# The first sum of every Strassen quarter on GpSimd instead of VectorE, in a one-core encoder trunk

## The chip, the cores and the metric
One core of one Trainium2 chip runs the whole program. The time is device microseconds (us) of one execution. The kernel before took 1798.45 us, the median of 3 runs (1797.22 to 1799.62).

## The reference, cut to what matters
The program computes a two-layer encoder trunk on x of shape (1, 256, 2048), all in float32: layer 0 is a pooling mixer and an MLP, then shared keys and values are made, layer 1 is a differential attention and an MLP, and a last normalization follows. The change lies in the two MLPs alone:

```
def sqrelu_mlp(h, w_in, w_out):        # h (1, 256, 2048)
    u = jax.nn.relu(h @ w_in)          # w_in  (2048, 8192)
    return (u * u) @ w_out             # w_out (8192, 2048)

for l in range(2):
    ...
    h = h + sqrelu_mlp(rms_norm(h, mlp_norm[l]), w_mlp_in[l], w_mlp_out[l])
```

Each MLP streams 134 MB of weights from HBM, and each weight is used for 256 tokens.

## The kernel before, in words
**Tiles.** The 8192 hidden columns of an MLP are cut into NP = 8 pairs of two strips of 512. For pair 0 the product h @ w_in is made plainly. For pairs 1 to 7 it is made by Strassen's scheme in the Winograd form: the tokens (2 x 128), the rows of the weights (two halves) and the columns (two strips) make 2 x 2 blocks, and seven products stand in for eight. Each pair is done in four **units** (k = 0 to 3, the quarters of the inner dimension). A unit loads four pieces a, b, c, d of 128 x 1024 float32 (512 KB each) into `raw_half[0]`. The seven right-hand operands of a unit are a, c, d and four sums, made in place: b = a + b, then d = d + b, a = d - a, c = c + d.

**Exactness.** TensorE multiplies float32r values. So each operand is split into a high part (`w_hi`, a rounding copy by ScalarE, L560 or L566) and a low part (`w_lo = raw - w_hi`, by VectorE, L960), and each product is three matmuls: hi*hi, hi*lo, lo*hi. One 128 x 1024 operand split in this way is a **lot**; `w_hi` and `w_lo` have 8 slots, used in turn. Behind the seven lots of a unit come four lots of `w_out` for the pair before (`out_lot`, two calls, each of which splits two lots: L554 on ScalarE, L952/L954 on VectorE), whose products go to the output.

**Who does what.** SP issues the loads; a and b of the next unit are issued when the sixth lot of this one is split (`in_unit`, L441, L436). ScalarE makes the high parts, seeds and drains PSUM banks. VectorE makes all four sums of a unit (L967, L976, L979, L981), the low parts, the recombinations of Strassen's products (`c_11`, L1051, and `c_rest`, L1057 to L1067) and the low parts of the hidden activations (`u_low`, L1074). TensorE runs the products (L1508 to L1510 into fresh banks, L1514 to L1516 onto seeded ones) and the transposes of the hidden tiles (L1543, once for each pair). GpSimd makes only the reciprocal roots of the norms.

**Order.** Every engine has one list in program order, written by hand, and counters (semaphores) hold it. `lo_ready` counts lots that are split, `pe_done` lots that TensorE has used, `w_summed` the sums. The second sum of a unit (L976) waits for the first by `w_summed`, and so does ScalarE's high part of b (`hi_sum`, L566). On VectorE the first sum (L967) stands at the head of each unit, behind the two `out_lot` calls of the unit before, and in unit 0 behind `c_rest`. On one **round** (one pair), VectorE's list is: c_11 of the pair; out lots; c_rest; first sum, lots and sums of unit 0 with `u_low` between them; out lots; units 1, 2 and 3 in the same way.

Of the kernel before, what the change touches and what calls it, by code (L numbers as in the profile page):

```python
# [26 lines left out]
ALU = mybir.AluOpType  # L27
# [10 lines left out]
RAW = 4  # L38
# [12 lines left out]
NP = FF // (2 * SW)  # L51
# [83 lines left out]
def trunk(nc, x, pool_w, pool_scale, w_kv, w_q, lam, w_o,  # L135
          w_mlp_in, w_mlp_out, final_norm, keep_consts, pool_consts, out):
    with ExitStack() as ctx:
# [3 lines left out]
        def sem(name):  # L141
            return ctx.enter_context(nc.semaphore(name))
# [47 lines left out]
        def place(at, *shape):  # L190
            n = int(np.prod(shape))
            ap = arena[:, at:at + n]
            if len(shape) == 2:
                ap = ap.rearrange("p (a b) -> p a b", b=shape[1])
            if len(shape) == 3:
                ap = ap.rearrange("p (a b c) -> p a b c", b=shape[1], c=shape[2])
            return ap
# [37 lines left out]
        raw_half = (raw, place(0, RAW, 2, SW))  # L235
# [24 lines left out]
        raw_landed = [sem(f"raw_landed{i}") for i in range(2 * RAW)]  # L260
# [27 lines left out]
        w_summed = sem("w_summed")  # L288
# [77 lines left out]
        def i_at(layer, p):  # L366
            if isinstance(p, int) and p == 0:
                return MLP_AT[layer]
            return p * 44 + (MLP_AT[layer] - 28)
# [7 lines left out]
        def i_landed(layer, p, i):  # L377
            if isinstance(p, int) and p == 0:
                return LANDED[layer][i % 2] + i // 2 + 1
            return p * 4 + (LANDED[layer][0] - 2 + i + 1)  # L380
# [133 lines left out]
        @block.gpsimd  # L514
        def _(pool):
            nc.gpsimd.memset(x_ssq[:, :, 0:4], 0.0).then_inc(sums_cleared, 1)
            nc.gpsimd.memset(x_ssq[:, :, 4:5], EPS).then_inc(sums_cleared, 1)
            nc.gpsimd.memset(neg_half[:], -0.5).then_inc(half_set, 1)
            pool.wait_ge(half_set, 1)

            def inv_rms(k):
                pool.wait_ge(mean_done, k + 1)
                nc.gpsimd.tensor_tensor(rms[:, k, :], mean[:, k, :], neg_half[:, 0:TB], ALU.pow).then_inc(rms_done, 1)

            for k in range(3):
                inv_rms(k)
            for t in range(PAIRS):
                pool.wait_ge(o_mean_done, t + 1)
                nc.gpsimd.tensor_tensor(o_rms[:, t, :], o_mean[:, t, :], neg_half[:], ALU.pow).then_inc(o_rms_done, 1)
            inv_rms(3)  # L530
            for tb in range(TB):
                pool.wait_ge(mean_done, 5 + tb)
                nc.gpsimd.tensor_tensor(rms[:, 4, tb:tb + 1], mean[:, 4, tb:tb + 1], neg_half[:, 0:1], ALU.pow).then_inc(rms_done, 1)
# [398 lines left out]
        def _(dve):  # L932
# [26 lines left out]
                dve.wait_ge(hi_ready, at + 1)  # L959
                nc.vector.tensor_tensor(w_lo[:, slot], raw_half[half][:, i], w_hi[:, slot].bitcast(F32), ALU.subtract).then_inc(lo_ready, 1)  # L960

            def t1_sum(half, landed):

                a, b = raw_half[half][:, 0], raw_half[half][:, 1]
                dve.wait_ge(raw_landed[RAW * half], landed * 16)
                dve.wait_ge(raw_landed[RAW * half + 1], landed * 16)
                nc.vector.tensor_tensor(b, a, b, ALU.add).then_inc(w_summed, 1)  # L967

            def mix_lo_lots(at, slot, half, sums, steps):

                a, b, c, d = (raw_half[half][:, i] for i in range(4))
                for step in steps:
                    if step == 3:
                        dve.wait_ge(w_summed, sums + 1)
                        dve.wait_ge(lo_ready, at + 3)
                        nc.vector.tensor_tensor(d, d, b, ALU.add).then_inc(w_summed, 1)  # L976
                    elif step == 4:
                        dve.wait_ge(w_summed, sums + 2)
                        nc.vector.tensor_tensor(a, d, a, ALU.subtract).then_inc(w_summed, 1)  # L979
                    elif step == 5:  # L980
                        nc.vector.tensor_tensor(c, c, d, ALU.add).then_inc(w_summed, 1)  # L981
                    lo_piece(at + step, (slot + step) % HALVES, half, (0, 2, 3, 1, 3, 0, 2)[step])
# [55 lines left out]
            def square_relu(layer, i):  # L1038

                buf, source = ((hid_12, B_P3), (hid_22, B_22))[i]  # L1040
                dve.wait_ge(pe_done, i_at(layer, 0) + 16)
                dve.wait_ge(rms_done, 2 * layer + 2)
                nc.vector.tensor_scalar(buf, source[:], rms[:, 2 * layer + 1, i:i + 1], 0.0, ALU.mult, ALU.max).then_inc(relu_dve, 1)
                dve.wait_ge(relu_dve, 2 * layer + i + 1)
                nc.vector.tensor_tensor(buf, buf, buf, ALU.mult).then_inc(hidden_dve, 1)

            def c_11(layer, p):

                dve.wait_ge(pe_done, i_at(layer, p) + 35)
                dve.wait_ge(p1_copied, p + 7 * layer)  # L1050
                nc.vector.tensor_tensor(hid_11, B_P2[:], p1_copy, ALU.add).then_inc(c_added, 1)  # L1051

            def c_rest(layer, p):

                done = (p + (7 * layer - 1)) * 7
                dve.wait_ge(pe_done, i_at(layer, p) + 38)
                nc.vector.tensor_tensor(hid_12, B_P6[:], p1_copy, ALU.add).then_inc(c_added, 1)  # L1057
                dve.wait_ge(pe_done, i_at(layer, p) + 39)
                dve.wait_ge(c_added, done + 2)
                nc.vector.tensor_tensor(hid_21, B_P7[:], hid_12, ALU.add).then_inc(c_added, 1)  # L1060
                dve.wait_ge(c_added, done + 3)
                nc.vector.tensor_tensor(hid_22, B_P5[:], hid_21, ALU.subtract).then_inc(c_added, 1)
                nc.vector.tensor_tensor(hid_12, B_P5[:], hid_12, ALU.subtract).then_inc(c_added, 1)
                dve.wait_ge(c_added, done + 5)
                nc.vector.tensor_tensor(hid_12, B_P3[:], hid_12, ALU.add).then_inc(c_added, 1)
                dve.wait_ge(pe_done, i_at(layer, p) + 40)
                nc.vector.tensor_tensor(hid_21, B_P4[:], hid_21, ALU.add).then_inc(c_added, 1)  # L1067

            def u_low(layer, p, last, bs=range(4)):

                for b in bs:
                    dve.wait_ge(u_rounded, (p + 8 * layer) * 4 + (b + 1))
                    hi, lo = u_tiles(2 * b, last)
                    nc.vector.tensor_tensor(lo, u_banks(p)[b][:].rearrange("p (c t) -> p c t", c=2), hi.bitcast(F32), ALU.subtract).then_inc(u_taken, 1)  # L1074
# [19 lines left out]
            def out_lot(layer, p, par, g, cd):  # L1094
                lo_pair(o_at(layer, p, g) + 2 * cd, (4 * par + LATER * layer + OUT_AT[g] + 2 * cd) % HALVES, 1, cd)

            def in_pair(layer, p, par):

                at, slot = i_at(layer, p), (4 * par + LATER * layer) % HALVES
                sums = p * 16 + (112 * layer - 16)  # L1100
                second = isinstance(p, int) and p == 1

                def unit(k, steps):
                    mix_lo_lots(at + UNIT_AT[k], (slot + UNIT_AT[k]) % HALVES, 0, sums + 4 * k, steps)

                for k in range(4):
                    if k == 0 and not second:
                        c_rest(layer, p - 1)
                    t1_sum(0, i_landed(layer, p, k))
                    if k == 0 and second:  # L1110
                        unit(0, range(6))
                        square_relu(layer, 0)
                        square_relu(layer, 1)
                        unit(0, (6,))
                        out_lot(layer, p - 1, par, 0, 0)
                        u_low(layer, p - 1, False)
                    elif k == 0:
                        unit(0, range(5))
                        u_low(layer, p - 1, False, (0, 1))
                        unit(0, (5,))  # L1120
                        u_low(layer, p - 1, False, (2, 3))
                        unit(0, (6,))
                    else:
                        unit(k, range(7))
                    if k == 3:
                        c_11(layer, p)
                    if not (k == 0 and second):
                        out_lot(layer, p - 1, par, k, 0)
                    if k == 3 and isinstance(p, int) and p == NP - 1:
                        c_rest(layer, p)  # L1130
                    out_lot(layer, p - 1, par, k, 1)
# [4 lines left out]
            def mlp(layer):  # L1136
# [14 lines left out]
                for p in (6, 7):  # L1151
                    in_pair(layer, p, (p + 1) % 2)
# [759 lines left out]
```

## Time and profile before
| | us |
|---|---|
| profiled execution, its own time | 1796.73 |
| its span | 1794.9 |
| TensorE busy | 1782.4 (99%) |
| VectorE busy | 1476.3 (82%) |
| ScalarE busy | 1199.6 (67%) |
| GpSimd busy | 13.0 (1%) |
| share of TensorE in the chain that ended last | 95% |

The span is the profiled part; the time of an execution is 1.83 us longer here. In the slices that belong to the two MLPs VectorE is busy at 8 or 9 tenths; in the attention between them at 5 to 7. TensorE's granted clock is full throughout. A matmul of 512 columns is shown with 390 ns, but the next begins 0.23 us after it, so busy times of single matmuls overlap.

### The profile page before, as it was taken

The page shows a single profiled execution, that of the slowest core. Times are in us where ns is not written, and L with a number is a line of the kernel's source. Part 1 is how long each engine was busy: PE and PEld are TensorE (multiplying, and loading weights), DVE is VectorE, ACT ScalarE, POOL GpSimd, SP SyncE. Part 2 cuts the span into 40 slices and gives each one's busy share as a digit, 9 for nine tenths or more (in the row PEclk, how much of TensorE's full clock was granted, in tenths as well). Part 3 has the DMA queues.
Part 4 walks back from the last instruction along what each step waited for, and adds up shares of the span by engine and source line. Part 5 has one row for each costly group of instructions (what it writes and reads, how often), then busy time and mean ns, then how long its engine had stood idle before and what let it go on. Part 6 is the DMA issues. An engine that isn't in the chain of part 4 may idle for free.

```text
span 1794.9 us, 23765 instructions
## 1 busy us (share of the span) xinstructions
PE 1782.4 (99%) x8118; PEld 1476.3 (82%) x8118; DVE 1476.3 (82%) x1495; ACT 1199.6 (67%) x1491; POOL 13.0 (1%) x17
## 2 busy tenths in 40 slices
PE   9999999999999999999999999999999999999998
PEld 7888888788888888888888888888888888888887
DVE  7888999899898987755557777889998989898976
ACT  7667777777777775633345545677777777767773
POOL 0000000000000000000000000000000000000000
PEclk9999999999999999999999999999999999999999
DMA  8545656465656555566654446455656565655562
GB/s 311 182 165 188 230 179 244 160 218 187 212 187 232 191 202 195 180 191 189 188 193 145 139 161 215 154 193 178 226 188 204 187 230 196 213 188 188 203 227 109
DMA packets 178656, 348.65 MB, mean 194 GB/s; under 512 B 10624, under 2 KB 10752, under 8 KB 178176
## 3 DMA queue, kind: packets, MB, share of 16 engines
q1 hardware_dynamic: 177984, 346.02, 56.8%
q10 hardware_dynamic: 576, 1.44, 0.2%
q8 instruction: 50, 0.82, 0.2%
q14 instruction: 46, 0.38, 0.1%
HBM read 345.32 MB, written 2.10 MB: 194 GB/s over the span
## 4 chain that ended last, share of the span: by engine, by line
PE 95%; DVE 1%; issue 1%; ACT 1%; DMA 1%; SPq 0%; DVEq 0%; POOL 0%; POOLq 0%; ACTq 0%
PE bank L1508 12%; PE bank L1509 12%; PE bank L1510 12%; PE bank L1514 12%; PE bank L1515 12%; PE bank L1516 12%; PE bank L1473 7%; PE bank L1475 6%; PE bank L1474 6%; PE bank L1543 1%; PE bank L1500 1%; DVE w_lo L954 0%; DMA h<-in_x 0%; DMA raw<-in_w_mlp_out 0%; PE bank L1822 0%
## 5 line engine op out<-in xcount | busy, mean ns | idle before, releaser
L960 DVE TENSOR_TENSOR w_lo<-raw,w_hi 128x1024 fp32r<-128x1024 f32 x392 | 469.0, 1218 | 2.4 <-ACT w_hi L560 0.4
L566 ACT ACTIVATE w_hi<-raw 128x1024 fp32r<-128x1024 f32 x224 | 236.9, 1058 | 225.3 <-DVE raw L976 139.2
L1514 PE MATMUL bank<-w_hi,u_hi_a 128*128 128x512 f32 x896 | 349.4, 390 | 1.6 <-ACT bank L676 1.0
L1516 PE MATMUL bank<-w_hi,u_lo_a 128*128 128x512 f32 x896 | 348.7, 389 | 0.0
L1515 PE MATMUL bank<-w_lo,u_hi_a 128*128 128x512 f32 x896 | 348.6, 389 | 0.0
L1508 PE MATMUL bank<-w_hi,mix_hi 128*128 128x512 f32 x828 | 324.3, 392 | 0.8 <-ACT h L684 0.6
L1510 PE MATMUL bank<-w_hi,mix_lo 128*128 128x512 f32 x828 | 322.4, 389 | 0.0
L1509 PE MATMUL bank<-w_lo,mix_hi 128*128 128x512 f32 x828 | 322.2, 389 | 0.0
L954 DVE TENSOR_TENSOR w_lo<-arena,w_hi 128x2048 fp32r<-128x2048 f32 x114 | 257.2, 2286 | 63.3 <-ACT w_hi L554 63.3
L543 ACT ACTIVATE w_hi<-raw 128x1024 fp32r<-128x1024 f32 x128 | 133.7, 1062 | 148.5 <-PE bank L1475 141.5
L554 ACT ACTIVATE w_hi<-arena 128x2048 fp32r<-128x2048 f32 x114 | 215.1, 1907 | 23.6 <-PE bank L1510 20.4
L938 DVE TENSOR_TENSOR w_lo<-raw,w_hi 128x1024 fp32r<-128x1024 f32 x128 | 153.3, 1220 | 72.7 <-ACT w_hi L543 72.3
L560 ACT ACTIVATE w_hi<-raw 128x1024 fp32r<-128x1024 f32 x168 | 174.7, 1054 | 46.6 <-DMA raw<-in_w_mlp_in 39.8
L1514 PEld LDWEIGHTS bank<-w_hi,u_hi_a 128*128 128x128 f32 x896 | 168.2, 188 | 39.2 <-issue 2.3
L1516 PEld LDWEIGHTS bank<-w_hi,u_lo_a 128*128 128x128 f32 x896 | 168.2, 188 | 35.1
L1515 PEld LDWEIGHTS bank<-w_lo,u_hi_a 128*128 128x128 f32 x896 | 168.2, 188 | 34.3
L1508 PEld LDWEIGHTS bank<-w_hi,mix_hi 128*128 128x128 f32 x828 | 155.5, 188 | 34.0 <-issue 1.3
L1510 PEld LDWEIGHTS bank<-w_hi,mix_lo 128*128 128x128 f32 x828 | 155.4, 188 | 32.5
L1509 PEld LDWEIGHTS bank<-w_lo,mix_hi 128*128 128x128 f32 x828 | 155.5, 188 | 31.4
L1475 PE MATMUL bank<-w_hi,a_lo 128*128 128x512 f32 x352 | 137.2, 390 | 0.0
L1473 PE MATMUL bank<-w_hi,a_hi 128*128 128x512 f32 x320 | 126.2, 394 | 0.0
L1474 PE MATMUL bank<-w_lo,a_hi 128*128 128x512 f32 x320 | 124.5, 389 | 0.0
(198 smaller groups left out, 2301.2 us busy)
## 6 DMA issues: line engine op xcount, KB each, us to landing
raw<-in_w_mlp_in SPq DMA_DIRECT2D x240, 512.0 KB, 4.9
arena<-in_w_mlp_out SPq DMA_DIRECT2D x240, 512.0 KB, 6.2
raw<-in_w_kv SPq DMA_DIRECT2D x64, 512.0 KB, 4.5
raw<-in_w_q SPq DMA_DIRECT2D x32, 512.0 KB, 4.6
raw<-in_w_o SPq DMA_DIRECT2D x32, 512.0 KB, 4.4
arena<-in_w_mlp_in SPq DMA_DIRECT2D x16, 512.0 KB, 6.3
raw<-in_w_mlp_out SPq DMA_DIRECT2D x16, 512.0 KB, 5.5
raw<-in_pool_w SPq DMA_DIRECT2D x4, 512.0 KB, 9.9
```

The costliest lines, as they stand in the source:

```text
L566: nc.scalar.activation(w_hi[:, slot], raw_half[half][:, i], ACT.Copy).then_inc(hi_ready, 1)
L954: nc.vector.tensor_tensor(w_lo[:, slot:slot + 2], raw_half[half][:, 2 * cd:2 * cd + 2], w_hi[:, slot:slot + 2].bitcast(F32), ALU.subtract) ...
L960: nc.vector.tensor_tensor(w_lo[:, slot], raw_half[half][:, i], w_hi[:, slot].bitcast(F32), ALU.subtract).then_inc(lo_ready, 1)
L1473: nc.tensor.matmul(banks[tb][:], hi[:, tok], w_hi[:, n, kk, :], start=begin, stop=False)
L1474: nc.tensor.matmul(banks[tb][:], hi[:, tok], w_lo[:, n, kk, :], start=False, stop=False)
L1475: last = nc.tensor.matmul(banks[tb][:], lo[:, tok], w_hi[:, n, kk, :], start=False, stop=end)
L1508: nc.tensor.matmul(bank[:], hi, w_hi[:, slot, kk, :], start=begin, stop=False)
L1509: nc.tensor.matmul(bank[:], hi, w_lo[:, slot, kk, :], start=False, stop=False)
L1510: return nc.tensor.matmul(bank[:], lo, w_hi[:, slot, kk, :], start=False, stop=end)
L1514: nc.tensor.matmul(bank[:], hi, w_hi[:, slot, kk, :], start=False, stop=False, skip_group_check=True)
L1515: nc.tensor.matmul(bank[:], hi, w_lo[:, slot, kk, :], start=False, stop=False, skip_group_check=True)
L1516: return nc.tensor.matmul(bank[:], lo, w_hi[:, slot, kk, :], start=False, stop=False, skip_group_check=True)
```

## The change
The first sum of each unit (b = a + b) is taken out of VectorE's list and given to GpSimd, which makes all 28 sums of a layer (pairs 1 to 7, four units each) in one row of instructions, each as soon as both pieces have landed. It keeps its semaphore. The other three sums stay on VectorE.

```diff
-            for k in range(3):
-                inv_rms(k)
+            def t1_sums(layer):
+
+                a, b = raw_half[0][:, 0], raw_half[0][:, 1]
+                for p in range(1, NP):
+                    for k in range(4):
+                        pool.wait_ge(raw_landed[0], i_landed(layer, p, k) * 16)
+                        pool.wait_ge(raw_landed[1], i_landed(layer, p, k) * 16)
+                        nc.gpsimd.tensor_tensor(b, a, b, ALU.add).then_inc(w_summed, 1)
+
+            inv_rms(0)
+            inv_rms(1)
+            t1_sums(0)
+            inv_rms(2)
...
             inv_rms(3)
+            t1_sums(1)
...
-            def t1_sum(half, landed):
-
-                a, b = raw_half[half][:, 0], raw_half[half][:, 1]
-                dve.wait_ge(raw_landed[RAW * half], landed * 16)
-                dve.wait_ge(raw_landed[RAW * half + 1], landed * 16)
-                nc.vector.tensor_tensor(b, a, b, ALU.add).then_inc(w_summed, 1)
...
                 for k in range(4):
                     if k == 0 and not second:
                         c_rest(layer, p - 1)
-                    t1_sum(0, i_landed(layer, p, k))
```

GpSimd's list in the kernel before, whole behind its start; `rms` and `o_rms` are the roots of the norms:

```order
8 L518 MEMSET neg_half 128x4
9 L523 ISA
10 L523 TENSOR_TENSOR rms<-mean,neg_half 128x2 x3
11 L529 TENSOR_TENSOR o_rms<-o_mean,neg_half 128x4 x4
12 L523 TENSOR_TENSOR rms<-mean,neg_half 128x2
13 L533 TENSOR_TENSOR rms<-mean,neg_half 128x1 x2
```

The same place in the changed kernel (`raw` holds the pieces a and b):

```order
8 L518 MEMSET neg_half 128x4
9 L523 ISA
10 L523 TENSOR_TENSOR rms<-mean,neg_half 128x2 x2
11 L532 TENSOR_TENSOR raw<-raw 128x1024 x28
12 L523 TENSOR_TENSOR rms<-mean,neg_half 128x2
13 L540 TENSOR_TENSOR o_rms<-o_mean,neg_half 128x4 x4
14 L523 TENSOR_TENSOR rms<-mean,neg_half 128x2
15 L532 TENSOR_TENSOR raw<-raw 128x1024 x28
16 L545 TENSOR_TENSOR rms<-mean,neg_half 128x1 x2
```

The 28 sums of each layer stand between two roots of norms that lie before and after that MLP.

VectorE's list in the kernel before, from the last out lots of a unit (L954) to the second sum of the next (L976):

```order
146 L954 TENSOR_TENSOR w_lo<-arena,w_hi 128x2048
147 L965 ISA
148 L967 TENSOR_TENSOR raw<-raw 128x1024
149 L959 REGISTER_ALU
150 L960 TENSOR_TENSOR w_lo<-raw,w_hi 128x1024
151 L959 REGISTER_ALU
152 L960 TENSOR_TENSOR w_lo<-raw,w_hi 128x1024
153 L959 REGISTER_ALU
154 L960 TENSOR_TENSOR w_lo<-raw,w_hi 128x1024
155 L974 REGISTER_ALU
156 L976 TENSOR_TENSOR raw<-raw 128x1024
```

The same place in the changed kernel (its L966, L972 and L981 are L954, L960 and L976 of before):

```order
140 L966 TENSOR_TENSOR w_lo<-arena,w_hi 128x2048
141 L971 REGISTER_ALU
142 L972 TENSOR_TENSOR w_lo<-raw,w_hi 128x1024
143 L971 REGISTER_ALU
144 L972 TENSOR_TENSOR w_lo<-raw,w_hi 128x1024
145 L971 REGISTER_ALU
146 L972 TENSOR_TENSOR w_lo<-raw,w_hi 128x1024
147 L979 REGISTER_ALU
148 L981 TENSOR_TENSOR raw<-raw 128x1024
```

The low parts of a, c and d now follow the out lots directly; nothing else moved on VectorE.

## Rows read from the trace of the kernel before

**Rows 1.** The page: busy time of each engine, share of the span, instructions
```profile
PE 1782.4 (99%) x8118; PEld 1476.3 (82%) x8118; DVE 1476.3 (82%) x1495; ACT 1199.6 (67%) x1491; POOL 13.0 (1%) x17
```

**Rows 2.** Windows, one round in layer 0: engines' busy us, clock, DMA
```profile
425.68:509.10 83.42, 83.42 (x378) 69.19 (x377) 75.49 (x66) 63.15 (x74) 0.00 (x0) 1.00 0.57 201
```

**Rows 3.** Timeline of TensorE: start us, us, engine, line, operation [idle before]
```profile
340.08 0.38 PE L1543 MATMUL bank<-keep,arena 128*128 128x128 f32 x2
...
353.48 0.49 PE L1514 MATMUL bank<-w_hi,u_hi_a 128*128 128x512 f32 x1 [0.61 <-DVE w_lo L954]
...
425.68 0.38 PE L1543 MATMUL bank<-keep,arena 128*128 128x128 f32 x2
...
436.98 0.40 PE L1514 MATMUL bank<-w_hi,u_hi_a 128*128 128x512 f32 x1
...
509.10 0.38 PE L1543 MATMUL bank<-keep,arena 128*128 128x128 f32 x2
```

**Rows 4.** Timeline of VectorE over the round that begins at 425.68
```profile
434.40 2.35 DVE L952 TENSOR_TENSOR w_lo<-arena,w_hi 128x1024 fp32r<-128x1024 f32 x2
...
453.59 4.49 DVE L954 TENSOR_TENSOR w_lo<-arena,w_hi 128x2048 fp32r<-128x2048 f32 x2 [1.80 <-ACT w_hi L554]
458.00 1.22 DVE L967 TENSOR_TENSOR raw<-raw 128x1024 f32<-128x1024 f32 x1
459.14 3.48 DVE L960 TENSOR_TENSOR w_lo<-raw,w_hi 128x1024 fp32r<-128x1024 f32 x3
...
472.72 2.29 DVE L954 TENSOR_TENSOR w_lo<-arena,w_hi 128x2048 fp32r<-128x2048 f32 x1 [1.79 <-ACT w_hi L554]
...
492.81 0.69 DVE L1051 TENSOR_TENSOR arena<-bank,arena 128x512 f32<-128x512 f32 x1 [2.68 <-ACT arena L642]
493.42 4.48 DVE L954 TENSOR_TENSOR w_lo<-arena,w_hi 128x2048 fp32r<-128x2048 f32 x2
...
501.86 1.22 DVE L967 TENSOR_TENSOR raw<-raw 128x1024 f32<-128x1024 f32 x1
...
517.81 4.49 DVE L954 TENSOR_TENSOR w_lo<-arena,w_hi 128x2048 fp32r<-128x2048 f32 x2
```

**Rows 5.** Timeline of ScalarE, last lot of units 1 and 3 to their out lots
```profile
449.48 1.06 ACT L566 ACTIVATE w_hi<-raw 128x1024 fp32r<-128x1024 f32 x1
...
451.59 3.71 ACT L554 ACTIVATE w_hi<-arena 128x2048 fp32r<-128x2048 f32 x2
...
487.81 1.06 ACT L566 ACTIVATE w_hi<-raw 128x1024 fp32r<-128x1024 f32 x1
...
490.31 1.92 ACT L554 ACTIVATE w_hi<-arena 128x2048 fp32r<-128x2048 f32 x1 [0.19 <-PE bank L1510]
```

**Rows 6.** Timeline, GpSimd's small operations and VectorE beside the first
```profile
51.62 2.69 POOL L523 TENSOR_TENSOR rms<-mean,neg_half 128x2 f32<-128x2 f32 x1 [40.56 <-DVE mean L945]
...
1116.62 0.70 POOL L523 TENSOR_TENSOR rms<-mean,neg_half 128x2 f32<-128x2 f32 x1 [49.42 <-DVE mean L945]
```

**Rows 7.** The same stretch on VectorE
```profile
51.45 2.29 DVE L954 TENSOR_TENSOR w_lo<-raw,w_hi 128x2048 fp32r<-128x2048 f32 x1
53.66 0.69 DVE L1023 TENSOR_TENSOR arena<-arena 128x512 f32<-128x512 f32 x1
```

**Rows 8.** Groups of VectorE's instructions by form: count | busy us, mean ns | idle before
```profile
L954 DVE TENSOR_TENSOR w_lo<-arena,w_hi 128x2048 fp32r<-128x2048 f32 x114 | 257.2, 2286 | 63.3 <-ACT w_hi L554 63.3
...
L967 DVE TENSOR_TENSOR raw<-raw 128x1024 f32<-128x1024 f32 x56 | 68.2, 1217 | 0.7 <-issue 0.7
```

**Rows 9.** SP's issue of piece b of unit 1, and its landing
```profile
L436 SPq DMA_DIRECT2D raw<-in_w_mlp_in x1: 373/373/373, 451.2 to 451.2; - x1
...
DMA to landing us min/median/max: 4.6/4.6/4.6
```

**Rows 10.** Timeline, last pair: ScalarE's last square, TensorE's transposes behind it
```profile
668.63 0.64 ACT L657 ACTIVATE arena<-arena 128x512 f32<-128x512 f32 x1
...
670.42 0.27 PE L1543 MATMUL bank<-keep,arena 128*128 128x128 f32 x1
```

## The prediction, made before the changed kernel ran
> **What bounds the kernel now.** I read the busy shares first: TensorE is busy 1782.4 us of the span of 1794.9, VectorE 1476.3 [rows 1]. The whole upside of any change that leaves TensorE's work alone is therefore 12.5 us, start and tail included. Then one round of the MLP, by windows: in 83.42 us TensorE is busy for 83.42, VectorE for 75.49, at a granted clock of 1.00, the 2.4 GHz level [rows 2]. So VectorE looks as if it had 8 us to give in each round. The timelines say where that room is, and they say that it is not to be had.
>
> TensorE runs the out lots of unit 0 from 436.98; VectorE had their low parts ready at 434.40 + 2.35 = 436.75 [rows 3, 4]. In the round before, TensorE started the same work at 353.48 after waiting for that very VectorE line [rows 3]. The chain that gets there is VectorE's: c_11 at 492.81, out lots, c_rest, first sum at 501.86, unit 0, out lots at 517.81 [rows 4]. It takes 25.0 us.
>
> The rest of the round goes at VectorE's and ScalarE's own pace too. From the out lots of one unit to those of the next are 472.72 - 453.59 = 19.13 us [rows 4], while TensorE takes 20.4 for a unit (a unit is a quarter of the round's 360 matmuls of 512 columns; the 16 short transposes take the rest of the 83.42). The idle time of VectorE ahead of the out lots, 1.80 and 1.79 us, is ended by ScalarE, which can only begin when VectorE has made the last sum of that unit: it is part of the chain and no cover. The only place where this chain waits for TensorE is unit 3: ScalarE needs 490.31 - 487.81 = 2.50 us from the last lot to the out lots there, and 451.59 - 449.48 = 2.11 in unit 1 [rows 5]. The difference, 0.39 us a round, is the whole slack; the 2.68 us of idle before c_11 [rows 4] is otherwise ScalarE's work. VectorE with its waits on ScalarE is a second bound, half a per cent below TensorE.
>
> **The change part by part.** *Removed:* 56 sums of 1217 ns on VectorE [rows 8]; in its list each takes 459.14 - 458.00 = 1.14 us [rows 4], 4.56 a round, 64 us in all. Since TensorE is busy throughout, this is worth nothing where VectorE is on time. One round is longer than the others: 425.68 - 340.08 = 85.60 us against 83.42 [rows 2, 3], and that is where TensorE waited for VectorE. Up to 1.14 us of its 2.18 can come back. I count that only where the sum becomes free, below.
>
> *Added:* 56 sums of the same shape on GpSimd. When do they run? Piece b of unit 1 is issued at 451.2 and lands 4.6 us later, at 455.8 [rows 9]. VectorE is then inside two out-lot subtractions that run from 453.59 to 458.08 [rows 4]. Each reads two tensors from SBUF, as the new sum does.
>
> What the two engines do to one another is shown for a small operation only. GpSimd's root over 2 columns takes 0.70 us where VectorE is idle (1116.62). At 51.62 the same root took 2.69: it ended at 54.31, 0.57 us behind the end of a VectorE subtraction of 2.29 us that had begun at 51.45 [rows 6, 7]. So GpSimd's read of SBUF stands until VectorE's two-input instruction is over, and then gets its turn even though VectorE goes on without a gap at 53.66. That next instruction took a normal 0.69: two columns are too few to hold it up. 1024 columns are not, if the rule holds in both directions. I take it to hold: GpSimd gets its turn at the end of an out lot, and VectorE's next subtraction stands until GpSimd has read.
>
> How long? The trace has no wide operation of GpSimd. From below: one pass over 1024 columns at VectorE's pace, which is (2286 - 1217) for 1024 more columns [rows 8], 1.07 us. From above: two passes, one for each input, and the whole 0.70 of a small operation, 2.84 us. I take two passes through one port without the fixed part, 2.14 us, because GpSimd waits out its own start behind VectorE, as at 51.62. Net, VectorE's chain is longer by 2.14 - 1.14 = 1.00 us in each unit (bounds: shorter by 0.07, longer by 1.70).
>
> The Trainium skill states the rule in both directions: in "SBUF — State Buffer", section "Who interferes with whom", a VectorE instruction with two SBUF inputs and a GpSimd instruction that reads SBUF exclude one another for a whole instruction. The rows at 51.62 agree for GpSimd as the loser; for VectorE as the loser no row here shows it. In "GPSIMD Engine Reference", section "Performance versus the Vector engine", an addition of 2048 float32 columns is given as 4497 ns on GpSimd and 2293 on VectorE; the second agrees with the 2286 here. Half of 4497 would make the net 1.11 in place of 1.00, and by that estimate the sum below would be 52 us instead of 46.
>
> *Sum.* From the out lots of unit 0 in pair 1 to those in pair 7 are six rounds. Each becomes longer by 4 x 1.00 - 0.39 = 3.61 us, 21.7 together. In unit 0 GpSimd's turn comes between the two out-lot instructions that begin at 493.42, so c_rest also moves; the first sum that stood behind it at 501.86 is gone; net again 1.00. In the last pair units 1 to 3 are late by 3.00 - 0.39 = 2.61. ScalarE's last square ended at 669.27 and TensorE's transposes began at 670.42 [rows 10], a cover of 1.15, which leaves 1.5. That is 23.1 us for a layer and 46.2 for two. The own time of the profiled execution, 1796.7 (its span and 1.8 around it), becomes 1842.9. It lies 1.7 below the median of the runs, which would give 1844.7; I say 1844.
>
> *The moved waits.* ScalarE's high part of b and VectorE's second sum need the first sum. It would be ready at about 458.1 + 2.1 = 460.2, while VectorE still has a, c and d to split, 3.48 us of work that stood at 459.14 before [rows 4]. So these two waits cost nothing beyond the above. In GpSimd's list the root after MLP 0 stands behind 28 sums, the last of which precedes it by a whole last pair; no cost. SP has nothing new in its list, but its loads are released by the sixth lot of a unit and so come later with VectorE.
>
> **The rivals.**
> *1. GpSimd's reads do not hold VectorE* (or hold it for about one pass). For it: VectorE's 0.69 at 53.66 beside GpSimd's tail. Against it: GpSimd itself plainly stood. Then VectorE's chain is shorter by up to 1.14 a unit, TensorE is busy anyway, and about 1.1 us of the long round returns: 1797 by the runs, no change. A gain of more than 3.6 us would need TensorE's idle time in the MLPs, which is not there.
> *2. GpSimd loses every turn while VectorE goes on without a gap*, and reads only when VectorE stands at the second sum for want of the first. Then VectorE waits there for two passes and the fixed 0.70, net 2.84 - 1.14 = 1.70 a unit. Six rounds of 6.8 - 0.39 and a last part of 5.1 - 0.39 - 1.15 are 42 a layer, 84 in all: 1882. Against it: at 51.62 it got its turn between two instructions. The same number is the upper bound of the forecast.
> *3. The hold is short* (1.2 to 1.7 us, partly shared): a net of 0.1 to 0.5 a unit, 0 to 20 us in all, 1799 to 1819. It decides from 0.1 a unit, where the 0.39 of a round is used up.
> *4. The change doesn't unload VectorE in time:* the sum comes later than VectorE reaches L976. That needs GpSimd to take over 4 us for it; then each unit waits, with the price of rival 2 or more.
>
> **How the numbers follow.** Forecast (turns in both directions, 1820 to 1870): 0.60. Rival 1: 0.20. Rival 2 with 4: 0.09. Rival 3: 0.11. Range for 8 in 10: 1803 to 1874; below it lies rival 1 and the weakest part of 3, above it most of rival 2. A measurement here tells about 0.2% (3.6 us) from no change. Slower: 0.60 + 0.09 + most of rival 3 = 0.78. Within 0.2%: nearly all of rival 1 and a little of 3, 0.19. Faster: 0.03. The likeliest case's own range is 1820 to 1870.
>
> **What would show it.** Right: 56 GpSimd additions, each ending 2 us or more behind the end of a VectorE out-lot subtraction; the subtraction behind that one (L972 or the second L966) shown with about 3 us in place of 1.2, or begun 2 us late; units 20.1 us apart on VectorE instead of 19.1; TensorE's rounds near 87 us, with its waits before the out lots of unit 0. Wrong: VectorE's subtractions all at 1.22 and 2.29 us and rounds of 83.4 (rival 1); or VectorE idle ahead of the second sum in every unit, released by GpSimd (rivals 2 and 4). If VectorE is held and yet TensorE's rounds stay at 83.4, my claim that the chain has only 0.39 us of slack is what failed.

## The result, and the profile after

The changed kernel takes 1841.05 us (median of 4 runs, 1840.66 to 1842.71) against 1798.63 for the kernel before (its median with a fourth run added), a ratio of 1.0239 with a 95% interval of 1.0227 to 1.0251. It is slower by 2.4%, by the mechanism forecast and to within 3 us of the forecast 1844. The span went from 1794.9 to 1840.9 us, 46.0 more; the sum had said 46.2.

The page of the changed kernel, busy time by engine and the shares of the chain that ended last (it answers to [rows 1]):

```profile
PE 1798.4 (98%) x8118; PEld 1473.4 (80%) x8118; DVE 1535.1 (83%) x1439; ACT 1198.4 (65%) x1491; POOL 220.3 (12%) x73
...
PE 71%; DVE 16%; issue 7%; ACT 4%; DMA 1%; DVEq 0%; ACTq 0%; SPq 0%; POOL 0%; POOLq 0%
```

56 instructions were taken from VectorE, and its busy time rose by 59 us. In the chain TensorE's share fell from 95% to 71%, and VectorE's is now 16%.

Which VectorE instructions became longer is seen in the groups by form (count | busy us, mean ns | idle before). L966, L972 and L964 are L954, L960 and L952 of the kernel before; L532 is the new addition on GpSimd:

```profile
L972 DVE TENSOR_TENSOR w_lo<-raw,w_hi 128x1024 fp32r<-128x1024 f32 x392 | 538.8, 1397 | 1.7
L966 DVE TENSOR_TENSOR w_lo<-arena,w_hi 128x2048 fp32r<-128x2048 f32 x114 | 292.5, 2596 | 65.0 <-ACT w_hi L566 65.0
...
L964 DVE TENSOR_TENSOR w_lo<-arena,w_hi 128x1024 fp32r<-128x1024 f32 x28 | 50.6, 1847 | 0.0
...
L532 POOL TENSOR_TENSOR raw<-raw 128x1024 f32<-128x1024 f32 x56 | 207.3, 3701 | 1027.0 <-DMA raw<-in_w_mlp_in 1027.0
```

Against 1218, 2286 and 1217 ns before [rows 8 for the second], these three groups took 392 x 0.179 + 114 x 0.310 + 28 x 0.630 = 123 us more, 2.2 us for each of GpSimd's 56 sums. The other forms of VectorE kept their means within a few ns. The mean hides that a few instructions took it all. The same lines by smallest, median and largest duration in ns:

```profile
L972 DVE TENSOR_TENSOR w_lo<-raw,w_hi x392: 1208/1217/3442, 76.0 to 1769.7; 128x1024 fp32r<-128x1024 f32 x196
L966 DVE TENSOR_TENSOR w_lo<-arena,w_hi x114: 2276/2286/4521, 46.8 to 1814.2; 128x2048 fp32r<-128x2048 f32 x114
```

A held subtraction takes 3442 - 1217 = 2.22 us longer. Taken one by one in the trace, each of the 56 additions of GpSimd has exactly one such subtraction beside it (32 of L972, 16 of L966, 8 of L964), and no other is longer than usual. The timeline of VectorE shows it in one round (with [rows 4]):

```profile
449.30 2.35 DVE L964 TENSOR_TENSOR w_lo<-arena,w_hi 128x1024 fp32r<-128x1024 f32 x2
451.57 2.28 DVE L966 TENSOR_TENSOR w_lo<-arena,w_hi 128x2048 fp32r<-128x2048 f32 x1
453.77 5.70 DVE L972 TENSOR_TENSOR w_lo<-raw,w_hi 128x1024 fp32r<-128x1024 f32 x3
...
469.58 4.49 DVE L966 TENSOR_TENSOR w_lo<-arena,w_hi 128x2048 fp32r<-128x2048 f32 x2 [1.80 <-ACT w_hi L566]
473.99 5.69 DVE L972 TENSOR_TENSOR w_lo<-raw,w_hi 128x1024 fp32r<-128x1024 f32 x3
...
489.78 2.29 DVE L966 TENSOR_TENSOR w_lo<-arena,w_hi 128x2048 fp32r<-128x2048 f32 x1 [1.80 <-ACT w_hi L566]
491.99 4.56 DVE L964 TENSOR_TENSOR w_lo<-arena,w_hi 128x1024 fp32r<-128x1024 f32 x2
...
511.15 6.70 DVE L966 TENSOR_TENSOR w_lo<-arena,w_hi 128x2048 fp32r<-128x2048 f32 x2
...
536.62 4.48 DVE L966 TENSOR_TENSOR w_lo<-arena,w_hi 128x2048 fp32r<-128x2048 f32 x2
```

GpSimd in the same round, and the shortest of the 56 additions:

```profile
122.88 2.40 POOL L532 TENSOR_TENSOR raw<-raw 128x1024 f32<-128x1024 f32 x1 [28.20 <-DMA raw<-in_w_mlp_in]
...
452.60 3.52 POOL L532 TENSOR_TENSOR raw<-raw 128x1024 f32<-128x1024 f32 x1 [24.22 <-DMA raw<-in_w_mlp_in]
471.96 4.37 POOL L532 TENSOR_TENSOR raw<-raw 128x1024 f32<-128x1024 f32 x1 [15.84 <-DMA raw<-in_w_mlp_in]
492.11 3.36 POOL L532 TENSOR_TENSOR raw<-raw 128x1024 f32<-128x1024 f32 x1 [15.78 <-DMA raw<-in_w_mlp_in]
512.35 3.36 POOL L532 TENSOR_TENSOR raw<-raw 128x1024 f32<-128x1024 f32 x1 [16.87 <-DMA raw<-in_w_mlp_in]
```

Read the two together. At 452.60 GpSimd's instruction begins while VectorE's out lot runs to 453.85, stands until then, and ends at 456.12, 2.27 us after it (2.24 to 2.29 us in all 56). VectorE's next subtraction is shown from 453.77 and is the held one: the three take 5.70 us where 3.48 is normal. A held instruction is shown as busy, not as waiting. From one unit's out lots to the next are now 489.78 - 469.58 = 20.20 us, where they were 19.13.

One round by windows (it answers to [rows 2]) and TensorE's waits in the whole program (us in total, times, longest):

```profile
437.28:524.59 87.31, 84.75 (x377) 68.88 (x376) 79.76 (x62) 62.80 (x74) 14.61 (x4) 1.00 0.56 192
```

```profile
PE bank L1512 <- ACT h L696: 17.2, 12, 1.6
PE bank L1518 <- DVE w_lo L966: 4.4, 12, 0.6
PE bank L1512 <- DVE u_lo_a L1079: 3.8, 2, 2.0
PE bank L1518 <- DVE w_lo L964: 2.8, 4, 0.7
```

The round is 87.31 us in place of 83.42 at the same granted clock of 1.00, and TensorE is idle for 2.6 of it by its records. The largest wait is for ScalarE, at the second product of unit 0; L1518 belongs to the out lots, and its two rows for VectorE are 7.2 us together.

### The profile page after: what moved, and what is told of

The parts are those of the page before. It is cut to its first block, busy times and chain, and to the rows that moved or that the text cites. A ratio compares the mean times of both kernels' runs of the same rounds, so it can differ in the third digit from the quotient of the medians.

```text
span 1840.9 us, 23739 instructions
## 1 busy us (share of the span) xinstructions
PE 1798.4 (98%) x8118; PEld 1473.4 (80%) x8118; DVE 1535.1 (83%) x1439; ACT 1198.4 (65%) x1491; POOL 220.3 (12%) x73
## 4 chain that ended last, share of the span: by engine, by line
PE 71%; DVE 16%; issue 7%; ACT 4%; DMA 1%; DVEq 0%; ACTq 0%; SPq 0%; POOL 0%; POOLq 0%
PE bank L1512 9%; PE bank L1514 8%; PE bank L1513 8%; PE bank L1518 8%; PE bank L1519 8%; PE bank L1520 8%; PE bank L1477 6%; PE bank L1479 6%; PE bank L1478 6%; DVE w_lo L972 6%; DVE w_lo L966 4%; ACT w_hi L578 1%; ACT w_hi L566 1%; PE bank L1504 1%; DVE u_lo_a L1079 1%
## 5 line engine op out<-in xcount | busy, mean ns | idle before, releaser
L972 DVE TENSOR_TENSOR w_lo<-raw,w_hi 128x1024 fp32r<-128x1024 f32 x392 | 538.8, 1397 | 1.7
L1518 PE MATMUL bank<-w_hi,u_hi_a 128*128 128x512 f32 x896 | 351.6, 392 | 10.5 <-DVE w_lo L966 4.4
L1512 PE MATMUL bank<-w_hi,mix_hi 128*128 128x512 f32 x828 | 328.6, 397 | 21.7 <-ACT h L696 17.2
L966 DVE TENSOR_TENSOR w_lo<-arena,w_hi 128x2048 fp32r<-128x2048 f32 x114 | 292.5, 2596 | 65.0 <-ACT w_hi L566 65.0
L532 POOL TENSOR_TENSOR raw<-raw 128x1024 f32<-128x1024 f32 x56 | 207.3, 3701 | 1027.0 <-DMA raw<-in_w_mlp_in 1027.0
L950 DVE TENSOR_TENSOR w_lo<-raw,w_hi 128x1024 fp32r<-128x1024 f32 x128 | 153.4, 1221 | 72.9 <-ACT w_hi L555 72.4
L1518 PEld LDWEIGHTS bank<-w_hi,u_hi_a 128*128 128x128 f32 x896 | 168.1, 188 | 55.5 <-issue 17.8
```

The costliest lines, as they stand in the source:

```text
L966: nc.vector.tensor_tensor(w_lo[:, slot:slot + 2], raw_half[half][:, 2 * cd:2 * cd + 2], w_hi[:, slot:slot + 2].bitcast(F32), ALU.subtract) ...
L1512: nc.tensor.matmul(bank[:], hi, w_hi[:, slot, kk, :], start=begin, stop=False)
L1518: nc.tensor.matmul(bank[:], hi, w_hi[:, slot, kk, :], start=False, stop=False, skip_group_check=True)
```

## Experiments

The theory: while GpSimd reads SBUF it holds VectorE's two-input instructions, for a time that goes with the columns it reads; and VectorE's chain has almost no slack, so that each hold comes out in the end. The rivals: a cost of the moved instruction as such (signal, start, order), and a chain with the slack that VectorE's busy time suggests.

### e1: GpSimd adds 8 columns instead of 1024

```diff
-                        nc.gpsimd.tensor_tensor(b, a, b, ALU.add).then_inc(w_summed, 1)
+                        nc.gpsimd.tensor_tensor(b[:, 0, 0:8], a[:, 0, 0:8], b[:, 0, 0:8], ALU.add).then_inc(w_summed, 1)
```

> GpSimd's instruction, its waits and its signal stay, but it adds only 8 of the 1024 columns (the first Strassen sum is left out but for these, so its values are wrong). Port theory (GpSimd's read holds VectorE's next two-input subtraction for 2.2 us because it reads 1024 columns twice): the hold goes with the columns to about 0.02 us, VectorE's chain is shorter than in the kernel before by 1.14 us a unit, TensorE is the bound: 1795 to 1799 us, no subtraction over 1.3 us per 1024 columns. Rival, a cost of the moved instruction itself (the semaphore, GpSimd's start of about 0.4 to 0.7 us, the order of the sums): the time stays above 1820 us.

Measured: 1793.64 us, ratio to the kernel before 0.9976 (0.9966 to 0.9985). That is 1.4 us below the lower end, and 47 us below the changed kernel, which has the same instructions, waits and signals in the same order. VectorE's subtractions have their old means:

```profile
L972 DVE TENSOR_TENSOR w_lo<-raw,w_hi 128x1024 fp32r<-128x1024 f32 x392 | 471.4, 1220 | 36.6 <-ACT w_hi L578 22.6 <-ACT w_hi L572 12.1
L966 DVE TENSOR_TENSOR w_lo<-arena,w_hi 128x2048 fp32r<-128x2048 f32 x114 | 257.9, 2288 | 74.4 <-ACT w_hi L566 74.4
```

So it is not the moved instruction as such that costs, but the columns that it works on. The run also says what the removal of the sum from VectorE is worth when it costs nothing elsewhere: 0.24%, small but clear of the interval.

### e2: 512 columns

```diff
+                        nc.gpsimd.tensor_tensor(b[:, 0, :], a[:, 0, :], b[:, 0, :], ALU.add).then_inc(w_summed, 1)
```

> As the changed kernel, but GpSimd adds only 512 of the 1024 columns (half of the first sum is left out). Port theory: the hold is half, 1.1 us, against 1.14 us taken off VectorE, net about 0 a unit: 1796 to 1802 us, and VectorE's held subtraction shown with about 2.3 us in place of 3.4. Rival, a fixed price of a turn: the hold stays near 2.2 us and the time near 1841. Rival, GpSimd's wide instruction holds VectorE only through a late sum: no stretched subtraction at all.

Measured: 1795.61 us, 0.9986 (0.9976 to 0.9996), 0.4 us below the range. Durations of VectorE's subtractions in ns, smallest, median, largest:

```profile
L972 DVE TENSOR_TENSOR w_lo<-raw,w_hi x392: 1209/1219/2332, 74.7 to 1720.8; 128x1024 fp32r<-128x1024 f32 x196
```

The hold is 2332 - 1219 = 1.11 us, half of 2.22 to the hundredth. There is no fixed part. The rival of a fixed price would have stayed near 1841 us.

### e3: the kernel before with one more subtraction a unit on VectorE

```diff
+                    if step == 2:
+                        spot = (slot + step) % HALVES
+                        dve.wait_ge(hi_ready, at + step + 1)
+                        nc.vector.tensor_tensor(w_lo[:, spot], raw_half[half][:, 3], w_hi[:, spot].bitcast(F32), ALU.subtract).then_inc(extra_done, 1)
+                        dve.wait_ge(extra_done, count)
                     lo_piece(at + step, (slot + step) % HALVES, half, (0, 2, 3, 1, 3, 0, 2)[step])
```

> The kernel before (all sums on VectorE) with one more subtraction of 128x1024 a unit on VectorE, the low part of d made twice, the second waiting for the first. About 1.3 us more a unit. If VectorE's chain has only 0.39 us of slack in a round: 2 x (6 x (5.2 - 0.39) + 3.9 - 1.54) = 62 us more, 1850 to 1865 us, TensorE's rounds near 88.2 us. Rival (VectorE, busy 75.5 of 83.4 us in a round, has 8 us to give): a round takes 5.2 us more VectorE work without being longer, 1797 to 1805 us, and GpSimd's effect in the changed kernel would need another explanation than VectorE's time.

Measured: 1857.83 us, 1.0335 (1.0317 to 1.0352), 59.9 us more than before. TensorE's transposes at the start of one round, and two rounds by windows:

```profile
443.61 0.49 PE L1549 MATMUL bank<-keep,arena 128*128 128x128 f32 x3
```

```profile
352.42:443.61 91.19, 86.64 (x377) 71.36 (x378) 83.55 (x71) 63.49 (x72) 0.00 (x0) 0.96 0.53 184
443.61:531.25 87.64, 84.80 (x378) 68.81 (x377) 79.96 (x70) 62.77 (x73) 0.00 (x0) 1.00 0.56 192
```

The second is a round of 87.64 us at a granted clock of 1.00; eight of the ten steady rounds lie between 87.6 and 88.2, near the 88.2 expected. The other two took 89.8 and 91.2. In the longest, TensorE stood for 4.5 us for ScalarE, and the granted clock was then 0.50, its 1.2 GHz level, from 360 to 366 us, so the mean is 0.96. Two shorter stretches at that level follow in layer 1. The three make 13.8 us, so up to 6.9 of the 59.9 us can be the clock's (an estimate: half of 13.8); the rounds at 1.00 don't have it in them. GpSimd has no part in this kernel. A unit takes about 1.27 us more on VectorE (475.85 to 496.25 from out lots to out lots, where [rows 4] has 19.13), and of 4 x 1.27 = 5.1 us a round 4.2 to 4.7 come out: VectorE's 8 us of idle time in a round are no slack. The share of busy time was the wrong view for that question.

### e4: one first sum a pair on GpSimd, beside instructions that read PSUM

```diff
-                for p in range(1, NP):
-                    for k in range(4):
+                for p in range(2, NP):
+                    for k in (0,):
+                        pool.wait_ge(lo_ready, i_at(layer, p))
```

VectorE keeps its `t1_sum` for all other units. GpSimd's wait lets it begin when the out lots ahead of c_rest are split.

> GpSimd makes the first sum only for unit 0 of pairs 2 to 7, and waits until the out lots ahead of c_rest are split, so that it runs beside c_rest, whose six instructions read one operand from PSUM and one from SBUF. All other first sums are on VectorE. Theory (only VectorE instructions with two SBUF inputs are held): GpSimd takes about 2.4 us, c_rest stays at 0.69 us an instruction, VectorE's chain is shorter by 1.14 us a round, TensorE is the bound: 1794 to 1798 us, the long round of 85.6 us cut by up to 1.1. Rival (GpSimd holds every VectorE instruction that reads SBUF): c_rest is stretched by 2.2 us, net 1.07 - 0.39 = 0.7 us a round more over 12 rounds, about 1805.

Measured: 1793.69 us, 0.9976 (0.9967 to 0.9986): 0.24% faster than the kernel before, 0.3 us below the range, and the same as e1, in which GpSimd reads nearly nothing. GpSimd's addition of one pair and VectorE beside it:

```profile
411.81 2.41 POOL L533 TENSOR_TENSOR raw<-raw 128x1024 f32<-128x1024 f32 x1 [80.95 <-DVE w_lo L967]
```

```profile
411.65 0.68 DVE L1070 TENSOR_TENSOR arena<-bank,arena 128x512 f32<-128x512 f32 x1
412.37 0.69 DVE L1073 TENSOR_TENSOR arena<-bank,arena 128x512 f32<-128x512 f32 x1
413.09 0.69 DVE L1075 TENSOR_TENSOR arena<-bank,arena 128x512 f32<-128x512 f32 x1
413.70 0.68 DVE L1076 TENSOR_TENSOR arena<-bank,arena 128x512 f32<-128x512 f32 x1
```

Neither is held: 2.41 us against 3.70 in the mean of the changed kernel, and 0.69 us for each instruction of c_rest, which reads one operand from PSUM and one from SBUF. All 12 additions take 2.41 to 2.43 us. Such instructions and GpSimd's reads don't exclude one another.

### e5 and e6: what in GpSimd's instruction holds

```diff
+                        nc.gpsimd.memset(b, 0.0).then_inc(w_summed, 1)
```

> As the changed kernel, but GpSimd writes zeros over b (1024 columns) in place of adding a to it: a write of the same width that reads nothing (the first sum is left out, its values are wrong). If what holds VectorE is GpSimd's reading: no VectorE subtraction over 1.3 us per 1024 columns, 1793 to 1795 us, as with 8 columns. Rival, GpSimd's write holds VectorE too, or any long GpSimd instruction does: subtractions stretched by about 1 us, 1795 to 1800 us.

```diff
+                        nc.gpsimd.tensor_scalar(b, b, 1.0, None, ALU.mult).then_inc(w_summed, 1)
```

> As the changed kernel, but GpSimd multiplies b by 1.0 in place: one input of 1024 columns instead of two (the first sum is left out). Theory (the hold is the time in which GpSimd reads, one pass for each input): hold 1.1 us an instruction, as with 512 columns of two inputs, 1795 to 1798 us, stretched subtractions of 2.3 us. Rival (the hold is the length of the instruction whatever it reads): it would follow GpSimd's own duration, and if that is near 2 us the time is above 1830.

Measured: e5 1793.75 us, 0.9975 (0.9966 to 0.9985); e6 1794.57, 0.9981 (0.9972 to 0.9991), 0.4 below the range. VectorE's subtraction and GpSimd's instruction by smallest, median and largest ns, in e5:

```profile
L972 DVE TENSOR_TENSOR w_lo<-raw,w_hi x392: 1211/1219/1228, 73.6 to 1717.2; 128x1024 fp32r<-128x1024 f32 x196
...
L532 POOL MEMSET raw<- x56: 952/956/967, 66.4 to 1701.9; 128x1024 f32 x56
```

and in e6:

```profile
L972 DVE TENSOR_TENSOR w_lo<-raw,w_hi x392: 1208/1218/2064, 74.5 to 1718.3; 128x1024 fp32r<-128x1024 f32 x196
...
L532 POOL TENSOR_SCALAR raw<-raw x56: 2772/3966/4859, 66.6 to 1704.0; 128x1024 f32<-128x1024 f32 x56
```

Writing 1024 columns holds nothing, and GpSimd is not held either (967 ns at most). Reading one input of 1024 columns holds VectorE for 2064 - 1218 = 0.85 us. This instruction is longer on GpSimd (2.77 us at least) than the addition is at its shortest (2.40), yet holds for less than half as long. So the hold goes with what GpSimd reads, not with the length of its instruction (GpSimd's durations are rough in a profile, but ScalarE stood 15 times for the end of this one). I had expected 1.1 us, one half of two passes; one pass alone is quicker than that.

### e7 and e8: which units

GpSimd makes the first sums of units 1 to 3 (e7), or of unit 0 alone and as soon as the pieces have landed (e8). The edit of e7; e8 has `(0,)` in its place, and both give `t1_sum` back to VectorE for the other units:

```diff
-                    for k in range(4):
+                    for k in (1, 2, 3):
```

> First sums of units 1, 2 and 3 on GpSimd, of unit 0 on VectorE. Theory (each sum on GpSimd is 2.22 - 1.14 = 1.08 us more on VectorE's chain, whatever the unit, less 0.39 a round): 3 x 1.08 - 0.39 = 2.85 us a round, 2 x (6 x 2.85 + 1.7) = 37.6 us, about 1835 us, rounds of 86.2 us. Rival (only unit 0's chain from c_11 to its out lots is critical, the leads of units 1 to 3 cover the rest): 1796 to 1800.

> First sum of unit 0 alone on GpSimd, as soon as its pieces have landed, units 1 to 3 on VectorE. It is the kernel that put it beside c_rest without the wait that put it there: GpSimd now reads between the two out lots. Theory: 1.08 - 0.39 = 0.69 us a round, 12 rounds, 8 us: 1803 to 1807 us, rounds of 84.1 us. Rival (unit 0's first sum is as cheap here as beside c_rest): 1793 to 1795.

Measured: e7 1829.78 us, 1.0178 (1.0161 to 1.0195), 31.9 more than before, 5.7 less than the 37.6 expected; e8 1807.28, 1.0052 (1.0035 to 1.0068), 9.4 more and 0.3 above its range. Together 41.3; the changed kernel with all four units has 42.4 more. The prices add up, also in units 1 to 3, where in the round of [rows 4] VectorE had the first out lots split 1.5 to 2.8 us before TensorE took them up (0.2 in unit 0). Two things were wrong in the expectations. Both sums were added to a kernel that itself loses 4.2 us against e1; against e1 the two cost 36.1 and 13.6 us. And the rounds of e8 are 84.4 to 84.7 us, not 84.1: the stretch with the hold takes 25.47 us for 24.39, and the 0.39 of unit 3 is not used (20.70 us, as before). That slack covers only holds in units 1 to 3. In e7, whose long rounds are 85.8 to 86.4 us for the 86.2 expected, it is used.

In e8 the first sum of unit 0 costs 13.6 us more than in e4. VectorE's out lots after c_11 show why:

```profile
494.86 0.69 DVE L1063 TENSOR_TENSOR arena<-bank,arena 128x512 f32<-128x512 f32 x1 [2.68 <-ACT arena L654]
495.47 6.69 DVE L966 TENSOR_TENSOR w_lo<-arena,w_hi 128x2048 fp32r<-128x2048 f32 x2
502.08 0.68 DVE L1069 TENSOR_TENSOR arena<-bank,arena 128x512 f32<-128x512 f32 x1
```

The two out lots take 6.69 us instead of 4.49, two microseconds ahead of the instructions that would have covered the same addition for nothing. (e8 has this also in pair 1, which e4 leaves to VectorE.)

### e9: four additions of 256 columns

```diff
+                        for j in range(2):
+                            for c in range(2):
+                                if 2 * j + c == 3:
+                                    pool.wait_ge(part_summed, 3 * (28 * layer + 4 * (p - 1) + k + 1))
+                                cols = slice(256 * c, 256 * c + 256)
+                                last = nc.gpsimd.tensor_tensor(b[:, j, cols], a[:, j, cols], b[:, j, cols], ALU.add)
+                                last.then_inc(part_summed if 2 * j + c < 3 else w_summed, 1)
```

> As the changed kernel, but each first sum is four GpSimd additions of 256 columns. Theory (the hold goes with the columns that GpSimd reads, 2.22 us for 1024): four holds of about 0.55 us on up to four of VectorE's subtractions, together again about 2.2 us a unit where all four meet one, so 1830 to 1845 us, and no subtraction over 1.9 us per 1024 columns. Rival (a long instruction is the trouble, short ones slip between): near 1794 to 1800 us. Rival (each turn has a fixed price, or four pieces come too late for the second sum): above 1850.

Measured: 1818.09 us, 1.0113 (1.0096 to 1.0130), 12 us below the theory's band and above the first rival's. VectorE and GpSimd in unit 1 of one round:

```profile
464.45 5.13 DVE L979 TENSOR_TENSOR w_lo<-raw,w_hi 128x1024 fp32r<-128x1024 f32 x3
470.21 1.22 DVE L988 TENSOR_TENSOR raw<-raw 128x1024 f32<-128x1024 f32 x1 [0.63 <-POOL raw L538]
```

```profile
462.41 7.76 POOL L538 TENSOR_TENSOR raw<-raw 128x256 f32<-128x256 f32 x4 [12.44 <-DMA raw<-in_w_mlp_in]
```

Three turns hold VectorE for 5.13 - 3.48 = 1.65 us, 0.55 each, as the theory has it. The fourth falls into a gap, but it is a gap that it makes: VectorE stands 0.63 us for the sum at the second sum. So a unit is no cheaper. What I missed is unit 0, where the later pieces run beside c_rest. VectorE's out lots at both ends of that stretch:

```profile
501.58 5.02 DVE L973 TENSOR_TENSOR w_lo<-arena,w_hi 128x2048 fp32r<-128x2048 f32 x2
...
525.37 4.48 DVE L973 TENSOR_TENSOR w_lo<-arena,w_hi 128x2048 fp32r<-128x2048 f32 x2
```

Only one turn meets an out lot (5.02 for 4.49 us); the other three cost nothing beside c_rest. The stretch takes 525.37 - 501.58 = 23.79 us where the changed kernel has 536.62 - 511.15 = 25.47, while units 1 to 3 take 20.26, 20.20 and 21.34, as they do there (20.28, 20.20, 21.37). From pair 2 on there are 12 such stretches, 12 x 1.68 = 20.2 of the 23.0 us between the two kernels. Where the rest lies is not shown.

## Why the prediction was right

*Mutual exclusion.* It rested on one direction only, GpSimd waiting for VectorE [rows 6, 7], and took the other from it. It holds in both: 56 sums, 56 held subtractions, 123 us on VectorE. The page "SBUF — State Buffer" of the Trainium skill, section "Who interferes with whom", says the same of the two kinds of instruction, and e4 and e5 agree with its limits (a VectorE instruction with one SBUF input, a GpSimd instruction that only writes). The page says too that the loser stands for the whole of the other's instruction. Here the measurement decides otherwise: in e6 the hold is 0.85 us beside a GpSimd instruction of 2.77 us or more.

*The size of the hold.* Estimated 2.14 us as two passes at VectorE's pace [rows 8], measured 2.22. The estimate was near for a reason that is only half right. A single pass takes 0.85 us, not 1.07, and two inputs take more than two such passes (2 x 0.85 = 1.70). 2.22 us is within 0.2 of the length of an undisturbed addition, 2.40, and GpSimd ends 2.24 to 2.29 us after the subtraction that it stood behind. So GpSimd probably reads for nearly all of that time, at its own pace; how the two inputs share it was not measured.

*The slack.* Claimed: 0.39 us a round [rows 5], though VectorE is idle for 8 us in 83 [rows 2]. e3 confirms it without GpSimd. By it four units cost 4 x (2.22 - 1.14) - 0.39 = 3.93 us; the round shown went from 83.42 to 87.31, 3.89 more. The place is right too. From one unit's out lots to the next's the round of [rows 4] has 19.19, 19.13, 20.70 and 24.39 us, and the changed kernel 20.28, 20.20, 21.37 and 25.47: 1.09, 1.07, 0.67 and 1.08 more. Only unit 3 gives something back, the 0.4 claimed.

*Where TensorE waits.* Forecast: ahead of the out lots of unit 0. Measured: 7.2 us ahead of out lots (4.4 and 2.8), but 17.2 at unit 0's second product, for ScalarE's drain of a bank (L696). That drain stands in ScalarE's list behind the high part that waits for VectorE's second sum. So it is the same lateness at an earlier door, and the sum did not depend on the door; but I had traced the chain to one consumer alone. The two moved waits cost nearly nothing, as forecast: VectorE never stood for GpSimd's sum, and ScalarE did six times, 3.2 us in all.

*Rival 1's gain.* I put the free case at 1.1 us, by the one long round, and said that more than 3.6 us was not to be had. e1, e4 and e5 gave 4.2 us, 0.24%: the prediction was wrong there. In none of their profiles is there a round over 83.4 us: of the long round the whole 2.2 us is gone, and the second rounds are 83.37 where they were 83.63. The rest lies in single hundredths a round and ahead of pair 1. The long round of the kernel before (85.60 us) is one of ten such rounds in its one profile. That it is an accident of that execution is unlikely: with 1796.73 us that execution is faster than every other recorded one of this kernel (1796.77 to 1800.39), while no run of e1, e4 or e5 is above 1794.28. So the kernel loses at least 2.4 us in every recorded execution; whether always by one long round stays open.

*The sum as a whole.* 46.2 us forecast in the span, 46.0 measured, and that near agreement is partly luck. With the hold of 2.22 the same sum gives 2 x (6 x 3.93 + 3.24 - 0.39 - 1.15) = 50.6 us. The gain that came back from the kernel before, 3.2 us in the profiles (1794.9 against 1791.7 in e1) and 4.2 in the runs, was counted as nothing. The two errors nearly cancel. Read from one pair's transposes to the next's, the forecast is 1.5 us more up to pair 1 and 3.6 for each of the six behind it. Measured in layer 1: 1.8, 2.7, 3.8, 3.9, 3.8, 3.6, 4.1. In layer 0: 3.5, 2.7, 3.9, 1.6, 3.9, 3.5, 4.3, where the 1.6 has the long round's 2.2 taken off. The 3.5 at its start holds a short stretch at a granted clock of 0.50 (99 to 101 us), after TensorE had stood for 2.0 us; by layer 1 that is 1.7 us of it.

## What to carry to other kernels

Before work is moved from VectorE to GpSimd, look at what VectorE runs while the moved instruction reads. Beside two-input SBUF instructions it costs VectorE the time of GpSimd's reads, here 2.22 us for a sum that took VectorE 1.14; beside instructions with one operand in PSUM it cost nothing (e4: 0.69 us each, as before), and a wait that puts it there is worth more than an early start (e4 against e8: 13.6 us, 0.8%).

The slack of an engine is not its idle share (here 0.39 us against 8 in a round). Follow its list through one period of the loop and count only the idle time that the bounding engine ends; idle time that another engine of the same chain ends is part of the chain.

## What was unexpected of the hardware

A held VectorE instruction is shown as begun right behind the one before it and with a longer duration, 3442 ns for 1217, so the waits' view doesn't show the loss at all; only the spread of durations does. The hold goes with the columns GpSimd reads, with nothing fixed (8 columns 0.00 us, 256 0.55, 512 1.11, 1024 2.22). One input of 1024 columns holds for 0.85 us, less than half of what two do. And a multiplication by a constant took GpSimd at least 2.77 us for 1024 columns, more than the 2.40 of an undisturbed addition of two tensors.
